# Expert pairs of a two-layer decoder: the four tile sums of the pair before placed behind the up products

## The chip, the cores and the metric

The kernel runs on one core of a Trainium2 chip. The metric is the device time of one execution in microseconds (us), lower is better. Each kernel is timed several times and the median is given; one further execution was recorded by the hardware profiler. The engines are TensorE (PE, with its weight loads shown as PEld), VectorE (DVE), ScalarE (ACT), GpSimd (POOL) and SyncE (SP), which issues the weight transfers.

## What is computed

Two decoder layers over 512 tokens of width 1024. Each layer has a token mixer (a gated linear recurrence in layer 0, sparse attention in layer 1), and then a mixture of 32 experts of which each token uses two. The change touches the experts alone. Cut to what matters:

```python
D_MODEL, SEQ, N_EXPERTS, TOP_K_IN_GROUP, D_EXPERT = 1024, 512, 32, 2, 512

def expert_block(args):
    xb, e = args
    return (jax.nn.silu(xb @ w_gate[e]) * (xb @ w_up[e])) @ w_down[e]

# x = x + sum over the token's two experts of gate * expert(rms_norm(x))
y = grouped_swiglu(xt, eid, w_gate, w_up, w_down).reshape(N, TOP_K_IN_GROUP, D)
out = jnp.sum(y * gate[..., None].astype(y.dtype), axis=1)
```

Every expert's weights are three matrices of 2 MiB in float32 (gate and up 1024x512, down 512x1024), so one layer reads 192 MiB of expert weights.

## The kernel before

**Pairs.** The experts of a layer are worked on in 16 pairs (`NP`), with up to 64 tokens (`CAP`) of each expert. The two experts sit in the two halves of the 128 partitions of PSUM. In each pair TensorE does: the gate product (`both` with `BANK_GATE`, 32 matmul records on L1646), the up product (`both` with `BANK_UP`, L1646), the transposes of the hidden values (`hidden_T`, L1654, 4 records), the transposes of the next pair's tokens (`tokens_T`, L1635, 8 records), and the down product (`down` on L1664, in the first two pairs of a layer `down_half` on L1673). In between it adds the outputs of the pair before to the tokens that they belong to: `combine` (L1682) multiplies a one-hot matrix with the outputs, split into three bf16 parts, for each of the four 128-token tiles: 6 matmuls of 512 columns per tile, 24 in all. `combine_of` does several tiles. They are written to PSUM banks 4 and 5 for tiles 0 and 2, banks 6 and 7 for tiles 1 and 3.

**VectorE.** `add_of` and `add_tile` (L2321) add each tile from PSUM to `x` in SBUF, and count `c_added`. A tile's matmuls wait until the tile two before it, which used the same banks, has been added. `hidden` (L2304) multiplies the up product with the silu of the gate product and counts `h_done`, for which `hidden_T` waits. `tokens_out` (L2298), `one_hot` (L2308) and the splitting of the outputs (L2314, L2317) come behind that.

**ScalarE.** It does the silu (L1188), copies the transposed hidden values to SBUF (L1192), for which the down product waits (`ht_sbuf`), and makes two of the three parts of the output.

**Weights.** SyncE's queue brings the six matrices of a pair (gate, up, down, of two experts each) into ten slots of `arena`, in the order in which they are used. A transfer into a slot is issued when the product that read the slot has finished (`slot_released`: `gate_psum`, `up_psum` or `y_psum`). The gate matrices of a pair go into the slots of the up matrices of two pairs before, the up matrices into those of the down matrices of two pairs before, the down matrices into those of the gate matrices of the pair before. For pairs 1 and 2 (the first twelve transfers beyond the ten slots) and again for the last two pairs of a layer, each matrix comes in two halves: L585 and L589. In the last two pairs the product waits for the second half at its middle (`late`), in the down product after a quarter.

**Ends.** In a layer's last pair there are no tokens to transpose. Its outputs are added behind the pair by the matmuls on L1756 and VectorE's L2365.

The order of every engine is written out by hand; nothing reorders it. The main loop of TensorE is unrolled, VectorE's pairs 2 to 14 run in a loop.

Of the kernel before, what the change touches and what calls it, by code (L numbers as in the profile page):

```python
# [283 lines left out]
def hybrid_trunk(nc, a, out):  # L284
# [8 lines left out]
    with ExitStack() as ctx:  # L293
# [198 lines left out]
        def wait_alone(eng, s, value):  # L492

            eng.wait_ge(s, value)
            eng.nop(nofuse=True)
# [4 lines left out]
        def wait_emptied(eng, name):  # L500
            who, n = jobs.emptied(name)
            eng.wait_ge(emptied[who], n)
# [40 lines left out]
        def landed_at(L, q):  # L543

            per_layer = [[32 if given_back_by_halves(v) else 16 for v in range(u, 6 * NP, NU)] for u in range(NU)]
            return L * sum(per_layer[q % NU]) + sum(per_layer[q % NU][:q // NU + 1])
# [688 lines left out]
        def _(pe):  # L1235
# [42 lines left out]
            for L in range(2):  # L1278
# [339 lines left out]
                def banks_emptied():  # L1618

                    n = jobs.number[f"{L}.first.1"]  # L1620
                    for who in ("act", "dve"):
                        pe.wait_ge(emptied[who], jobs.before[n][who])

                def table():
                    b = open_bank(f"{L}.table")
                    pe.wait_ge(placed, L + 1)
                    for k in range(2):
                        for t in range(NT):
                            ins = pe.matmul(b[:, 0:2 * NE], place_hot[:, k, t].rearrange("p c n -> p (c n)"),
                                            expert_pay[:, k, t].rearrange("p c e -> p (c e)"), start=k + t == 0, stop=k + t == NT)  # L1630
                    ins.then_inc(filled, 1)

                def tokens_T(s_, n=P):
                    for k in range(KD):
                        ins = pe.transpose(ps[:, BANK_XT[k // 4], (k % 4) * P:(k % 4) * P + n], xg[0:n, k::KD][:, 0:P], ident[0:n, 0:n])  # L1635
                    ins.then_inc(s_, 1)

                def both(bank, units, s_, spread=None, half=None, late=None):

                    for k in range(KD):  # L1640
                        if spread and k % 4 == 0:
                            wait_emptied(pe, spread[k // 4])
                        if late and k == KD // 2:
                            pe.wait_ge(late, 32 * (L + 1))
                        for e, u in enumerate(units):
                            ins = pe.matmul(ps[e * CAP:(e + 1) * CAP, bank, :], tokT[:, k, e * CAP:(e + 1) * CAP], rows_in[u][:, k, :],  # L1646
                                            start=k == 0, stop=k == KD - 1)
                        if half and k == KD // 2 - 1:
                            ins.then_inc(half, 1)
                    ins.then_inc(s_, 1)  # L1650

                def hidden_T(s_, n=P):
                    for j in range(KF):
                        ins = pe.transpose(ps[:, BANK_HT, j * P:j * P + n], h_sb[0:n, j::KF][:, 0:P], ident[0:n, 0:n])  # L1654
                    ins.then_inc(s_, 1)
# [22 lines left out]
                def combine(t, s_, part=slice(0, P)):  # L1678

                    for c in range(2):  # L1680
                        for q, y in enumerate(y_parts):
                            ins = pe.matmul(ps[:, 4 + 2 * (t % 2) + c, :], onehot[part, t * P:(t + 1) * P], y[part, c, :],  # L1682
                                            start=q == 0, stop=q == 2)
                    ins.then_inc(s_, 1)

                def combine_of(n, ts, started=True):

                    for t in ts:
                        if t == 0:
                            pe.wait_ge(m["y_mid"], n * 2 + 2)  # L1690
                            pe.wait_ge(m["y_low"], n * 2 + 2)
                            pe.wait_ge(m["g_done"], n + 1)
                        if started or t >= 2:
                            pe.wait_ge(m["c_added"], n * NT + (t - 1))
                        combine(t, m["c_psum"])

                def pair(p):

                    n, first, last = NP * L + p, p == 0, p == NP - 1
                    turned = (NP - 1) * L + p  # L1700
                    units = [(6 * p + j) % NU for j in range(6)]
                    half = half_read if p < 2 else None
                    late = [second_half[3 * (p - NP + 2) + v] if p >= NP - 2 else None for v in range(3)]

                    def weights_of(kind):
                        for j in (2 * kind, 2 * kind + 1):
                            pe.wait_ge(landed[units[j]], landed_at(L, 6 * p + j))

                    weights_of(0)
                    if first:  # L1710
                        for name in (f"{L}.rank.1", f"{L}.fT.{NT - 1}.0"):
                            wait_emptied(pe, name)
                        both(BANK_GATE, units[0:2], m["gate_psum"], [f"{L}.first.{h}" for h in range(2)], half=half)
                        banks_emptied()
                        table()
                    else:
                        pe.wait_ge(m["xt_sbuf"], turned * 2)
                        both(BANK_GATE, units[0:2], m["gate_psum"], half=half, late=late[0])
                        combine_of(n - 1, (0, 1), n > 1)
                    weights_of(1)  # L1720
                    both(BANK_UP, units[2:4], m["up_psum"], half=half, late=late[1])
                    if not first:
                        combine_of(n - 1, (2, 3))
                    wait_alone(pe, m["h_done"], n + 1)
                    hidden_T(m["ht_psum"])
                    if not first:
                        pe.wait_ge(m["c_added"], n * NT - 1)
                        if not last:
                            wait_alone(pe, gathered, (turned + 1) * 16)
                            tokens_T(m["xt_psum"])  # L1730
                    weights_of(2)
                    pe.wait_ge(m["ht_sbuf"], n + 1)
                    if first:
                        wait_emptied(pe, f"{L}.table")
                    if p >= 2:
                        down(units[4:6], m["y_psum"], late[2])
                        return
                    down_half(units[4:6], 0, (None, half))
                    if first:
                        wait_alone(pe, gathered, (turned + 1) * 16)  # L1740
                        tokens_T(m["xt_psum"])
                    down_half(units[4:6], 1, (m["y_psum"], m["y_psum"]))
# [47 lines left out]
        def _(dve):  # L1790
# [40 lines left out]
            for L in range(2):  # L1831
# [475 lines left out]
                def one_hot(c, s_, part=slice(0, P)):  # L2307
                    dve.tensor_scalar(onehot[part, :], iota_tok[part, :], c[part, 0:1], None, ALU.is_equal).then_inc(s_, 1)  # L2308
# [14 lines left out]
                def add_of(n, ts, started=True):  # L2323
                    for t in ts:
                        dve.wait_ge(m["c_psum"], n * NT + (t + 1))
                        if started:
                            dve.wait_ge(m["c_added"], n * NT + (t - 3))
                        add_tile(t, m["c_added"])

                def pair(n, p, first=False, second=False, last=False):  # L2330
                    dve.tensor_copy(cur[:], tabP[:, p, :] if isinstance(p, int) else
                                    tabP[:, bass.ds(p, 1), :].rearrange("p a b -> p (a b)")).then_inc(cur_ready, 1)
                    if not first:
                        add_of(n + (-1), (0, 1), not second)
                    dve.wait_ge(cur_ready, n + 1)
                    dve.wait_ge(m["up_psum"], n + 1)
                    dve.wait_ge(m["silu_done"], n + 1)
                    hidden(cur[:], m["h_done"])
                    if not first:
                        add_of(n + (-1), (2, 3), not second)  # L2340
                    if not last:
                        tokens_out(m["xt_psum"], n + (1 - L), m["xt_sbuf"])
                    one_hot(cur[:], m["g_done"])
                    if last:
                        last_split(n)
                    else:
                        split(m, n)
# [81 lines left out]
```

## Time and profile before

| | us |
|---|---|
| median of 3 runs | 1440.76 |
| lowest and highest | 1437.71, 1442.62 |
| the profiled execution | 1437.13 |
| its span in the trace | 1435.3 |
| TensorE (PE) busy | 1377.1 (96% of the span) |
| VectorE busy | 593.2 (41%) |
| ScalarE busy | 329.5 (23%) |

The span runs from the first to the last recorded instruction; 1.8 us lie around it. The profiled execution is 3.6 us under the median. TensorE worked at its full clock nearly everywhere (mean granted clock 0.997). The expert pairs of layer 0 run from about 253 to 711 us of the span and those of layer 1 from about 972 to the end. The kernel reads 457.41 MB from HBM.

### The profile page before, as it was taken

What the parts mean: (1) busy time and instruction counts of PE and PEld (TensorE: products, weight loads), DVE (VectorE), ACT (ScalarE), POOL (GpSimd) and SP (SyncE); (2) the same over time, 40 slices, a digit from 0 to 9 for tenths busy, and PEclk for the clock granted to TensorE, in tenths of its full rate; (3) what the DMA queues carried; (4) which work ended last, traced back from release to release, by engine and by line L of the source; (5) the groups of instructions that cost most, each with busy time, mean ns of one, the idle gap of its engine ahead of it and who ended that gap; (6) DMA issues with size and microseconds to landing.
All of it is one profiled execution on the core that took longest, in us unless ns stands there. A gap on an engine that the chain in (4) does not pass through costs nothing.

```text
span 1435.3 us, 16528 instructions
## 1 busy us (share of the span) xinstructions
PE 1377.1 (96%) x6368; PEld 619.6 (43%) x6433; DVE 593.2 (41%) x1112; ACT 329.5 (23%) x644; POOL 98.5 (7%) x191
## 2 busy tenths in 40 slices
PE   7999999999999999999899989999999999999997
PEld 3464466433333333333354555564343333333332
DVE  4655104434333333333539864244343333333333
ACT  4455002111111110111326764221111101100111
POOL 1001000200000000000000223003000000000000
PEclk9999999999999999999999999999999999999999
DMA  8207394999999999999930030699999999999995
GB/s 289 109 0 231 114 355 175 365 423 426 426 427 428 426 427 428 427 422 421 352 100 1 1 122 1 231 348 353 421 428 427 426 428 424 429 428 426 423 420 238
DMA packets 73999, 457.26 MB, mean 319 GB/s; under 512 B 15884, under 2 KB 23628, under 8 KB 43848
## 3 DMA queue, kind: packets, MB, share of 16 engines
q1 hardware_dynamic: 68160, 447.97, 76.6%
q0 software_dynamic: 4928, 8.22, 1.5%
q8 instruction: 53, 0.87, 0.2%
q10 hardware_dynamic: 840, 0.06, 0.0%
q14 instruction: 18, 0.15, 0.0%
HBM read 457.41 MB, written 10.53 MB: 326 GB/s over the span
## 4 chain that ended last, share of the span: by engine, by line
PE 70%; DMA 9%; SPq 8%; DVE 7%; ACT 3%; issue 2%; POOL 0%; DVEq 0%; ACTq 0%
PE ps L1646 22%; PE ps L1259 17%; PE ps L1664 11%; PE ps L1682 8%; DMA arena<-in_moe_w_up 5%; SPq L585 5%; DMA arena<-in_moe_w_down 4%; SPq L589 3%; PE ps L1673 2%; PE ps L1635 2%; DVE mix L1984 1%; DVE small L1983 1%; PE ps L1561 1%; PE ps L1520 1%; PE ps L1654 1%
## 5 line engine op out<-in xcount | busy, mean ns | idle before, releaser
L1646 PE MATMUL ps<-arena,xT 128*64 128x512 f32 x2048 | 454.5, 596 | 14.0 <-issue 11.3
L1646 PEld LDWEIGHTS ps<-arena,xT 128*64 128x64 f32 x2048 | 149.5, 137 | 298.5 <-issue 293.5
L2321 DVE TENSOR_TENSOR x<-ps,x 128x1024 f32<-128x1024 f32 x120 | 146.5, 1224 | 204.3 <-PE ps L1682 202.0
L1664 PE MATMUL ps<-arena,xT 128*64 128x512 f32 x896 | 199.1, 596 | 2.2 <-ACT xT L1192 1.6
L1259 PE MATMUL ps<-xT,arena 128*128 128x512 f32 x384 | 169.0, 595 | 1.7 <-DVE xT L1817 1.3
L1682 PE MATMUL ps<-mix,xT 128*128 128x512 bf16 x660 | 157.4, 379 | 6.4 <-issue 4.6
L1682 PEld LDWEIGHTS ps<-mix,xT 128*128 128x128 bf16 x720 | 65.5, 98 | 119.5 <-issue 48.7
L1664 PEld LDWEIGHTS ps<-arena,xT 128*64 128x64 f32 x896 | 61.8, 137 | 118.4 <-issue 112.0
L1259 PEld LDWEIGHTS ps<-xT,arena 128*128 128x128 f32 x384 | 71.9, 190 | 91.2 <-issue 88.5
L1192 ACT ACTIVATE xT<-ps 128x512 f32<-128x512 f32 x32 | 19.1, 597 | 390.6 <-PE ps L1654 390.6
L1259 PE MATMUL ps<-arena,mix 128*128 128x512 f32 (+1 forms) x256 | 105.6, 568 | 0.0
L2314 DVE TENSOR_TENSOR mix<-ps,mix 128x512 f32<-128x512 f32 x60 | 41.5, 691 | 151.9 <-ACT mix L1198 151.9
L2304 DVE SCALAR_TENSOR_TENSOR xT<-ps,cur,xT 128x512 f32<-128x512 f32 x32 | 24.0, 751 | 180.3 <-PE ps L1646 175.6
L1198 ACT ACTIVATE mix<-ps 128x512 bf16<-128x512 f32 x60 | 35.8, 597 | 204.8 <-PE ps L1664 175.3
L1259 PEld LDWEIGHTS ps<-arena,mix 128*128 128x128 f32 x256 | 47.9, 190 | 49.9 <-issue 48.8
L811 POOL CAST whole<-tabP 128x1 int32 (+1 forms) x30 | 5.7, 192 | 865.9 <-PE ps L1635 676.0
L1188 ACT ACTIVATE xT<-ps 128x512 f32<-128x512 f32 x32 | 19.1, 597 | 179.4 <-PE ps L1646 179.4
L804 POOL TENSOR_SCALAR arena<-arena,small 128x256 f32<-128x256 f32 (+3 forms) x80 | 39.4, 512 | 250.5 <-DVE small L1999 181.1
L1826 DVE TENSOR_TENSOR x<-ps,x 128x512 f32<-128x512 f32 x16 | 11.1, 692 | 92.5 <-PE ps L1259 89.4
L2298 DVE TENSOR_TENSOR xT<-ps,gains 128x512 f32<-128x512 f32 x60 | 38.6, 686 | 17.0 <-PE ps L1635 13.1
L2317 DVE TENSOR_TENSOR mix<-mix 128x512 bf16<-128x512 f32 x60 | 41.2, 687 | 2.9
L1201 ACT ACTIVATE mix<-mix 128x512 bf16<-128x512 f32 x60 | 37.5, 626 | 7.2 <-DVE mix L2314 7.2
(281 smaller groups left out, 1181.8 us busy)
## 6 DMA issues: line engine op xcount, KB each, us to landing
arena<-in_moe_w_gate SPq DMA_DIRECT2D x48, 2048.0 KB, 27.4
arena<-in_moe_w_up SPq DMA_DIRECT2D x48, 2048.0 KB, 26.2
arena<-in_moe_w_down SPq DMA_DIRECT2D x48, 2048.0 KB, 30.0
arena<-in_moe_w_down SPq DMA_DIRECT2D x32, 1024.0 KB, 20.6
arena<-in_moe_w_gate SPq DMA_DIRECT2D x32, 1024.0 KB, 21.4
arena<-in_moe_w_up SPq DMA_DIRECT2D x32, 1024.0 KB, 21.4
arena<-in_w_out SPq DMA_DIRECT2D x4, 2048.0 KB, 11.2
arena<-in_dsa_w_in SPq DMA_DIRECT2D x1, 5120.0 KB, 17.6
```

Of the source, the lines that this page charges most:

```text
L585: sp.dma_start(rows_in[u][:, ks, :], src[:, ks, :]).then_inc(done, 16)
L589: sp.dma_start(rows_down[u][:, js, :], src[:, js, :]).then_inc(done, 16)
L804: ins = pool.tensor_scalar(buf[:, h, 0:width], buf[:, h, 0:width], inv[:, h:h + 1], 1.0, ALU.mult, ALU.mult)
L1201: act.activation(y_mi[part, c, :], y_rest[part, c, :], ACT.Copy).then_inc(q["y_mid"], 1)
L1259: ins = pe.matmul(b[part, cols], l, r, start=i == 0, stop=i == len(pairs) - 1)
L1646: ins = pe.matmul(ps[e * CAP:(e + 1) * CAP, bank, :], tokT[:, k, e * CAP:(e + 1) * CAP], rows_in[u][:, k, :], start=k == 0, stop=k == KD - 1)
L1664: ins = pe.matmul(ps[e * CAP:(e + 1) * CAP, BANK_Y + c, :], hT[:, j, e * CAP:(e + 1) * CAP], rows_down[u][:, j, c * 512:(c + 1) * 512], st ...
L1682: ins = pe.matmul(ps[:, 4 + 2 * (t % 2) + c, :], onehot[part, t * P:(t + 1) * P], y[part, c, :], start=q == 0, stop=q == 2)
L2298: dve.tensor_tensor(tokT[:, 4 * q:4 * q + 4, :], ps[:, BANK_XT[q], :].rearrange("p (k n) -> p k n", k=4), gains[:, 3 * L + 2, 4 * q:4 * q ...
L2314: dve.tensor_tensor(y_rest[part, c, :], ps[part, BANK_Y + c, :], y_hi[part, c, :], ALU.subtract).then_inc(q["y_rest"], 1)
L2317: dve.tensor_tensor(y_lo[part, c, :], y_rest[part, c, :], y_mi[part, c, :], ALU.subtract).then_inc(q["y_low"], 1)
L2321: dve.tensor_tensor(x[:, t, :], ps[:, b:b + 2, :].rearrange("p a n -> p (a n)"), x[:, t, :], ALU.add).then_inc(s_, 1)
```

## The change

On TensorE the tiles 0 and 1 of the pair before move from between the gate and the up product to behind the up product, ahead of tiles 2 and 3. On VectorE the additions of tiles 0 and 1 move behind `hidden`. Nothing is added or removed.

```diff
--- before.py
+++ after.py
@@ -1716,10 +1716,10 @@
                     else:
                         pe.wait_ge(m["xt_sbuf"], turned * 2)
                         both(BANK_GATE, units[0:2], m["gate_psum"], half=half, late=late[0])
-                        combine_of(n - 1, (0, 1), n > 1)
                     weights_of(1)
                     both(BANK_UP, units[2:4], m["up_psum"], half=half, late=late[1])
                     if not first:
+                        combine_of(n - 1, (0, 1), n > 1)
                         combine_of(n - 1, (2, 3))
                     wait_alone(pe, m["h_done"], n + 1)
                     hidden_T(m["ht_psum"])
@@ -2330,13 +2330,12 @@
                 def pair(n, p, first=False, second=False, last=False):
                     dve.tensor_copy(cur[:], tabP[:, p, :] if isinstance(p, int) else
                                     tabP[:, bass.ds(p, 1), :].rearrange("p a b -> p (a b)")).then_inc(cur_ready, 1)
-                    if not first:
-                        add_of(n + (-1), (0, 1), not second)
                     dve.wait_ge(cur_ready, n + 1)
                     dve.wait_ge(m["up_psum"], n + 1)
                     dve.wait_ge(m["silu_done"], n + 1)
                     hidden(cur[:], m["h_done"])
                     if not first:
+                        add_of(n + (-1), (0, 1), not second)
                         add_of(n + (-1), (2, 3), not second)
                     if not last:
                         tokens_out(m["xt_psum"], n + (1 - L), m["xt_sbuf"])
```

TensorE's order in the last pair of layer 0, from the gate product's second half to the transposes of the hidden values, before (the names in brackets are the semaphores waited for; `second_half4` is the landing of the up matrices' second half):

```order
L1646 MATMUL ps<-arena,xT 64x512 x7
L1682 MATMUL ps<-mix,xT 128x512 [waits g_done,c_added,y_low,y_mid]
L1682 MATMUL ps<-mix,xT 128x512 x5
L1682 MATMUL ps<-mix,xT 128x512 [waits c_added]
L1682 MATMUL ps<-mix,xT 128x512 x5
L1646 MATMUL ps<-arena,xT 64x512 [waits landed3,landed2]
L1646 MATMUL ps<-arena,xT 64x512 x7
L1646 MATMUL ps<-arena,xT 64x512 [waits second_half4]
L1646 MATMUL ps<-arena,xT 64x512 x7
L1682 MATMUL ps<-mix,xT 128x512 [waits c_added]
L1682 MATMUL ps<-mix,xT 128x512 x5
```

The same place in the changed kernel:

```order
L1646 MATMUL ps<-arena,xT 64x512 x7
L1646 MATMUL ps<-arena,xT 64x512 [waits landed3,landed2]
L1646 MATMUL ps<-arena,xT 64x512 x7
L1646 MATMUL ps<-arena,xT 64x512 [waits second_half4]
L1646 MATMUL ps<-arena,xT 64x512 x7
L1682 MATMUL ps<-mix,xT 128x512 [waits g_done,c_added,y_low,y_mid]
L1682 MATMUL ps<-mix,xT 128x512 x5
L1682 MATMUL ps<-mix,xT 128x512 [waits c_added]
L1682 MATMUL ps<-mix,xT 128x512 x5
L1682 MATMUL ps<-mix,xT 128x512 [waits c_added]
L1682 MATMUL ps<-mix,xT 128x512 x5
```

The block of tiles 0 and 1 has gone from ahead of the up product to behind it, and tile 2, which waits for the addition of tile 0, now follows it at once.

VectorE's order in the last pair of layer 0, as a difference between the two kernels (in the rest of the loop it is the same move):

```order
 L2331 COPY cur<-tabP 128x2
-L2321 TENSOR_TENSOR x<-ps,x 128x1024 [waits c_added,c_psum] x2
 L2304 SCALAR_TENSOR_TENSOR xT<-ps,cur,xT 128x512 [waits silu_done,up_psum,cur_ready]
-L2321 TENSOR_TENSOR x<-ps,x 128x1024 [waits c_added,c_psum] x2
+L2321 TENSOR_TENSOR x<-ps,x 128x1024 [waits c_added,c_psum] x4
 L2308 TENSOR_SCALAR xT<-iota_tok,cur 128x512
```

All four additions now stand behind the hidden product of L2304.

## Rows read from the trace of the kernel before

**Rows 1.** The page's slices: DMA busy tenths and GB/s, 40 slices of 35.9 us

```profile
DMA  8207394999999999999930030699999999999995
GB/s 289 109 0 231 114 355 175 365 423 426 426 427 428 426 427 428 427 422 421 352 100 1 1 122 1 231 348 353 421 428 427 426 428 424 429 428 426 423 420 238
```

**Rows 2.** Windows: busy us of PE, PEld, DVE, ACT, POOL, PEclk, DMA share, GB/s

```profile
240.00:260.00 20.00, 19.70 (x133) 13.70 (x131) 12.14 (x47) 4.91 (x8) 0.00 (x0) 1.00 0.65 240
300.00:320.00 20.00, 19.84 (x96) 7.19 (x97) 7.51 (x11) 3.41 (x6) 1.20 (x2) 1.00 1.01 419
```

**Rows 3.** The page's DMA issues: count, KB of one, median us to landing

```profile
arena<-in_moe_w_down SPq DMA_DIRECT2D x48, 2048.0 KB, 30.0
```

**Rows 4.** Timeline of PE, pair 5 of layer 0: start us, us, what, idle before

```profile
390.56 7.04 PE L1646 MATMUL ps<-arena,xT 128*64 128x512 f32 x32
397.76 2.54 PE L1682 MATMUL ps<-mix,xT 128*128 128x512 bf16 x11 [0.16 <-issue]
400.22 7.09 PE L1646 MATMUL ps<-arena,xT 128*64 128x512 f32 x32
407.24 2.76 PE L1682 MATMUL ps<-mix,xT 128*128 128x512 bf16 x11
409.84 0.63 PE L1654 MATMUL ps<-ident,xT 128*128 128x128 f32 x4
...
411.30 7.09 PE L1664 MATMUL ps<-arena,xT 128*64 128x512 f32 x32
418.22 2.31 PE L1646 MATMUL ps<-arena,xT 128*64 128x512 f32 x10
```

**Rows 5.** Timeline of DVE in the same pair

```profile
399.12 2.52 DVE L2321 TENSOR_TENSOR x<-ps,x 128x1024 f32<-128x1024 f32 x2 [5.56 <-PE ps L1682]
407.42 0.75 DVE L2304 SCALAR_TENSOR_TENSOR xT<-ps,cur,xT 128x512 f32<-128x512 f32 x1 [5.77 <-PE ps L1646]
408.84 2.43 DVE L2321 TENSOR_TENSOR x<-ps,x 128x1024 f32<-128x1024 f32 x2 [0.67 <-PE ps L1682]
```

**Rows 6.** Timeline of pair 0, where TensorE waits for VectorE

```profile
269.26 0.75 DVE L2304 SCALAR_TENSOR_TENSOR xT<-ps,cur,xT 128x512 f32<-128x512 f32 x1 [2.29 <-issue]
...
270.16 0.72 PE L1654 MATMUL ps<-ident,xT 128*128 128x128 f32 x4 [1.01 <-DVE xT L2304]
```

**Rows 7.** Timeline of PE, layer 0: gate product of pair 12, gate and up of 13

```profile
588.22 7.09 PE L1646 MATMUL ps<-arena,xT 128*64 128x512 f32 x32 [2.19 <-issue]
...
618.72 7.09 PE L1646 MATMUL ps<-arena,xT 128*64 128x512 f32 x32 [2.03 <-issue]
...
629.16 7.09 PE L1646 MATMUL ps<-arena,xT 128*64 128x512 f32 x32 [0.67 <-DMA arena<-in_moe_w_up]
```

**Rows 8.** Timeline of PE and PEld, last pair of layer 0

```profile
686.16 7.33 PE L1646 MATMUL ps<-arena,xT 128*64 128x512 f32 x32
...
689.83 0.20 PEld L1646 LDWEIGHTS ps<-arena,xT 128*64 128x64 f32 x4 [0.90 <-DMA arena<-in_moe_w_up]
...
693.42 2.76 PE L1682 MATMUL ps<-mix,xT 128*128 128x512 bf16 x11
...
696.02 0.63 PE L1654 MATMUL ps<-ident,xT 128*128 128x128 f32 x4
```

**Rows 9.** The same timeline, down product of that pair and what follows

```profile
697.43 1.94 PE L1664 MATMUL ps<-arena,xT 128*64 128x512 f32 x8 [0.78 <-ACT xT L1192]
699.68 5.37 PE L1664 MATMUL ps<-arena,xT 128*64 128x512 f32 x24 [0.31 <-DMA arena<-in_moe_w_down]
704.98 2.76 PE L1756 MATMUL ps<-mix,xT 128*128 128x512 bf16 x11
```

**Rows 10.** Timeline of PE, last pair of layer 1

```profile
1411.44 2.76 PE L1682 MATMUL ps<-mix,xT 128*128 128x512 bf16 x11
...
1415.45 1.94 PE L1664 MATMUL ps<-arena,xT 128*64 128x512 f32 x8 [0.78 <-ACT xT L1192]
1417.66 5.37 PE L1664 MATMUL ps<-arena,xT 128*64 128x512 f32 x24 [0.27 <-DMA arena<-in_moe_w_down]
```

## The prediction, made before the changed kernel ran

> **What bounds the kernel now.** I read the page's slices first. TensorE looks full (96%), but so does the DMA: in both stretches of expert pairs nearly every slice has 9 tenths and about 427 GB/s [rows 1]. The windows of 20 us say when it starts: share 0.65 from 240 to 260 us, and 1.01 with 419 GB/s from 300 to 320 [rows 2]. So from pair 0 on the transfers run without a pause, and the time of their last landing is set by bytes over rate, not by TensorE.
>
> The timeline of a pair shows how close TensorE is to that. In pair 5 it never waits: from gate product to gate product 418.22 - 390.56 = 27.66 us [rows 4]. The stream needs more for a pair. In pair 13 the gate product waits 2.03 us and the up product 0.67 us [rows 7]. Gate products 12 and 13, which both wait, start 618.72 - 588.22 = 30.5 us apart [rows 7]. So TensorE starts a layer with ten loaded slots, works faster than they are refilled, and meets the stream at pair 11: by its own pace that gate product would come at 418.22 + 5 x 27.66 = 556.5 us, by the stream's at 588.22 - 30.5 = 557.7. From there each product starts when its weights land.
>
> The last pair is therefore the place that counts. The second half of the up matrices lands at 689.83 us, TensorE goes on at once, and tiles 2 and 3 start 3.59 us later, at 693.42 us [rows 8]. Behind them stand the transposes (696.02 us), ScalarE's copy, and the down product at 697.43 us. That reaches its first wait after a quarter and goes on at 699.68 us, when the last weights of the layer have landed [rows 8, 9]. A product takes 704.98 - 699.68 = 5.30 us for three quarters, so a quarter is 1.77 us. TensorE was ready for the last landing at 697.43 + 1.77 = 699.20 us and had **0.48 us to spare**. In layer 1 it is 1417.66 - 1415.45 - 1.77 = 0.44 us [rows 10]. Whatever is put between the last up product and the last down product beyond this half microsecond is paid in full.
>
> **The change, part by part.**
>
> Pairs 1 to 14, TensorE. Two tiles leave the place between gate and up and come back behind up: 400.22 - 397.76 = 2.46 us gone, 2.60 us (407.24 to 409.84) added, and the gap of 0.16 us before the first tile goes along with it [rows 4]. What is new is that tile 2 follows tile 1 at once and needs the banks of tile 0. VectorE starts adding tile 0 1.36 us after the first tile's matmuls start (397.76 to 399.12) and takes 1.26 us (2.52 for two) [rows 4, 5]. TensorE sees the end of a VectorE operation about 0.15 us later (269.26 + 0.75 to 270.16) [rows 6]. So tile 2 can start 1.36 + 1.26 + 0.15 = 2.77 us after tile 0 did, and the two tiles fill 2.54 us: a wait of 0.23 us. Tile 3 needs tile 1's addition, which ends 1.26 us after tile 0's, while tile 2's matmuls take 1.27 us: no second wait. I take 0.23 us; the bounds are 0 and 1.26, a whole addition laid open.
>
> Trainium skill, Perfetto Trace Analysis, section Optimizing Tensor Performance: independent matmul groups should rotate through different banks so that the evacuation of one overlaps the matmuls of the next. By that rule alone two pairs of banks would hide each addition and the wait would be zero, which takes 0.5 us off the sum below; the rows above leave 0.23 us per pair.
>
> VectorE's product for the hidden values comes 0.18 us after the up product and takes 0.75 us [rows 5], so it is done before the first tile is complete; putting it ahead of the additions delays nobody. The transposes, which wait for it, now have four tiles ahead of them instead of two.
>
> A pair thus takes 27.66 + 0.23, about 27.9 us, still under the stream's 30.5. Over ten pairs TensorE comes some 2 us later to the stream and gains 2.6 us in each pair behind it. Cost: nothing, as long as the stream never runs dry. The slots of the up matrices come free 2.5 us earlier, those of the down matrices up to 2 or 3 us later. A transfer of two matrices lasts about 9.8 us (689.83 to 699.67, [rows 8, 9]) and the median from issue to landing of a down matrix is 30.0 us [rows 3]: some 20 us of work stand ahead of it in the queue, more than the lateness. In the first pairs the queue is shorter, but so is the lateness (0.23 us for each pair).
>
> Last pair, TensorE. Does the up product still end when it did? The up product of pair 13 starts with its weights at 629.16 us [rows 7]; two pairs of 27.9 us later is 684.96, its half is done at 688.5, 1.3 us before the second half lands at 689.83. So its end stays at 693.42 us, tied to the landing. Behind it now stand 0.16 + 2 x 2.60 + 0.23 = 5.59 us instead of 2.60: **2.99 us more**. The 0.48 us to spare is used up, so the down product starts 2.99 us later, finds all its weights, and ends 2.99 - 0.48 = 2.51 us later. What it would do without the slack is 2.99, with no wait for an addition 2.28.
>
> In layer 1 the down matrices' second half lands at 1417.66 us; 9.84 us before that, 1407.82, plus 3.59 is 1411.41, against 1411.44 in the row [rows 10]. So here too the up product cannot end earlier, and the sum is 2.99 - 0.44 = 2.55, less the 0.03: 2.52 us.
>
> What follows the pairs (L1756, the last additions, in layer 0 the whole of layer 1) hangs on the end of the down product, and moves with it. Nothing on POOL's or SP's queue is moved; the next tokens are fetched once per pair as before.
>
> Sum: 2.51 + 2.52 = **5.0 us more**. Against the profiled execution's own 1437.13 us that is 1442.1. The runs' median is 3.6 us above it and I lay the sum on that: 1440.76 + 5.0 = **1445.8 us**, 0.35% slower. With no wait and with 0.5 us more wait for each of the two blocks the sum is 4.6 and 6.0.
>
> **Rivals.**
>
> *Hidden after all (not slower).* In the last pair there are 0.48 us to spare because the last two transfers land 9.84 us apart. If in the executions that make up the median the last down matrices came 3 us later after the up matrices than in the profiled one, the four tiles would vanish behind them. For it: the median run is 3.6 us longer, somewhere. Against: both layers show the same slack, 0.48 and 0.44 us, and a stream that is slow everywhere stretches 9.84 us by hundredths. It decides at 3.0 us; the time would be 1440.8 to 1443.
>
> *The additions hold TensorE up in every pair (much slower).* If tiles 2 and 3 each wait longer, say 1 us per pair in all, ten pairs make 10 us, TensorE reaches pair 11 some 9 us behind the stream (it came there 1.2 us ahead), and regains only 30.5 - 28.7 = 1.8 us per pair, 7 in four. Then it is late at the last up product too. It decides at about 0.8 us per pair; at 1 us each layer loses 3.0 + 0.8 - 0.5 + 2, some 5.5 us, so about 1452. Against it: VectorE's additions are as quick as the tiles (1.26 against 1.27 us).
>
> *A faster stream (faster).* The gate matrices are asked for 2.5 us earlier. The most that could give is the lack of rate in the first windows, 427 - 419 GB/s over some 40 us, 0.7 us in each layer [rows 2]. With the above it leaves +3.6 us, 1444.4. Only if the tail's cost is wrong as well would the kernel get faster.
>
> **How the numbers follow.** The forecast has 0.72, hidden 0.12, much slower 0.10, faster stream 0.06. A measurement of this kernel can tell about 0.3%, 4.3 us, from no change. The forecast's 4.6 to 6.0 lies just above that, and medians of a few runs with a spread of 5 us move by 1 to 2: two in three that it shows as slower, one in three as same. So slower is 0.48 + 0.10, and a little of the last, 0.59; same is 0.24 + 0.11 + 0.02, 0.37; faster 0.04. The range takes the forecast with its bounds and scatter and part of each neighbour: 1441 to 1449.5.
>
> **What would show it right or wrong.** In the changed kernel's timeline: gate to gate 27.9 us in pairs 2 to 10; a wait of some 0.2 us inside the 24 matmuls of L1682; the wait before the up product in pairs 11 to 13 grown to about 2 us and that before the gate product shrunk; DMA share still 1.0 with the last landing at the same place; the last down product with no wait for its weights, starting 7.0 us behind the end of the up product instead of 4.0, with L1756 2.5 us later in layer 0 and 5 us later in layer 1. It is wrong if the last down product still waits for its weights, if the DMA pauses in pairs 1 to 4, or if the additions cost TensorE over 0.8 us per pair.

## The result, and the profile after

| | us |
|---|---|
| changed kernel, median of 9 runs | 1445.72 (1442.90 to 1448.43) |
| kernel before, median of 9 runs | 1440.82 (1437.58 to 1443.23) |
| ratio of the two | 1.0035, 95% interval 1.0025 to 1.0045 |
| profiled execution of the changed kernel | 1442.90, span 1441.1 |

The change costs 5.0 us (3.6 to 6.5 by the interval). The predicted time was 1445.8 us. Here and below the ratio is an estimate from all runs of both kernels and not the quotient of the two medians, so the two can differ by 0.1%; a cost in us is worked out from the ratio.

The page's slices show the same picture as [rows 1]: the DMA is as full, and moves as much.

```profile
DMA  8207294999999999999830030698999999999995
GB/s 285 111 0 228 105 363 173 359 422 427 426 426 428 424 428 427 427 422 421 341 98 1 1 122 1 222 351 357 422 427 426 427 428 426 426 427 427 424 420 216
```

The window from 300 to 320 us, to set beside [rows 2] (busy us of PE, PEld, DVE, ACT and POOL, granted clock, DMA share, GB/s):

```profile
300.00:320.00 20.00, 20.00 (x101) 7.78 (x101) 6.67 (x10) 3.54 (x6) 1.21 (x2) 1.00 1.01 420
```

So the transfers run from pair 0 to the last weights with no slice in which they pause, before and after.

TensorE's timeline in pair 9 of layer 0, a pair without a wait for weights, answers to [rows 4]:

```profile
503.08 13.90 PE L1646 MATMUL ps<-arena,xT 128*64 128x512 f32 x64
516.92 5.64 PE L1682 MATMUL ps<-mix,xT 128*128 128x512 bf16 x24
522.39 0.63 PE L1654 MATMUL ps<-ident,xT 128*128 128x128 f32 x4
...
523.85 7.09 PE L1664 MATMUL ps<-arena,xT 128*64 128x512 f32 x32
530.77 7.04 PE L1646 MATMUL ps<-arena,xT 128*64 128x512 f32 x32
```

Gate and up product are now one run of 64 records, the four tiles one run of 24. From gate to gate it is 530.77 - 503.08 = 27.69 us, where before had 27.66: only 0.03 us more. The 0.03 is a difference of two terms. The four tiles take 522.39 - 516.92 = 5.47 us, which is 0.25 more than the 2.62 and 2.60 us of the two blocks before (from the end of the gate product at 397.60 to 400.22, and 407.24 to 409.84 [rows 4]). Gate and up product take 13.84 us in one run, where before they took 7.04 + 7.02 = 14.06 in two.

VectorE's timeline in pair 5, to set beside [rows 5]. The hidden product comes 0.17 us after the first tile starts behind the up product (406.16), then two additions, a pause, and two more:

```profile
406.33 0.75 DVE L2304 SCALAR_TENSOR_TENSOR xT<-ps,cur,xT 128x512 f32<-128x512 f32 x1 [11.00 <-PE ps L1646]
407.76 2.52 DVE L2321 TENSOR_TENSOR x<-ps,x 128x1024 f32<-128x1024 f32 x2 [0.67 <-PE ps L1682]
410.63 2.43 DVE L2321 TENSOR_TENSOR x<-ps,x 128x1024 f32<-128x1024 f32 x2 [0.36 <-PE ps L1682]
```

In the pairs that wait for weights the wait has moved from ahead of the gate product [rows 7] to ahead of the up product, here in pair 12 of layer 0; before it, gate follows down at once:

```profile
590.98 7.04 PE L1646 MATMUL ps<-arena,xT 128*64 128x512 f32 x32
600.75 7.09 PE L1646 MATMUL ps<-arena,xT 128*64 128x512 f32 x32 [2.73 <-DMA arena<-in_moe_w_up]
```

The last pair of layer 0, PE, PEld and one row of VectorE, answers to [rows 8, 9]:

```profile
692.05 3.65 PE L1646 MATMUL ps<-arena,xT 128*64 128x512 f32 x16 [1.23 <-DMA arena<-in_moe_w_up]
695.63 5.55 PE L1682 MATMUL ps<-mix,xT 128*128 128x512 bf16 x24
...
697.14 2.52 DVE L2321 TENSOR_TENSOR x<-ps,x 128x1024 f32<-128x1024 f32 x2 [0.58 <-PE ps L1682]
698.42 0.98 PEld L1682 LDWEIGHTS ps<-mix,xT 128*128 128x128 bf16 x6 [0.52 <-DVE x L2321]
...
699.71 0.98 PEld L1682 LDWEIGHTS ps<-mix,xT 128*128 128x128 bf16 x6 [0.32 <-DVE x L2321]
...
701.02 0.63 PE L1654 MATMUL ps<-ident,xT 128*128 128x128 f32 x4
...
702.43 7.09 PE L1664 MATMUL ps<-arena,xT 128*64 128x512 f32 x32 [0.78 <-ACT xT L1192]
...
709.45 2.76 PE L1756 MATMUL ps<-mix,xT 128*128 128x512 bf16 x12
```

The reader is to see three things. The up product still waits for its second half (1.23 us), so it ends where the landing lets it. The four tiles take 701.02 - 695.63 = 5.39 us. And the down product is one run of 32 records: it no longer waits for the last weights.

The last pair of layer 1 is the same, beside [rows 10]:

```profile
1411.34 3.65 PE L1646 MATMUL ps<-arena,xT 128*64 128x512 f32 x16 [1.10 <-DMA arena<-in_moe_w_up]
1414.93 5.55 PE L1682 MATMUL ps<-mix,xT 128*128 128x512 bf16 x24
...
1421.73 7.09 PE L1664 MATMUL ps<-arena,xT 128*64 128x512 f32 x32 [0.78 <-ACT xT L1192]
1428.75 2.76 PE L1756 MATMUL ps<-mix,xT 128*128 128x512 bf16 x12
```

**The tail** is the stretch from the landing of the last up weights to the first matmul of L1756. It was 704.98 - 689.83 = 15.15 us in layer 0; it is 709.45 - 692.05 = 17.40 and 1428.75 - 1411.34 = 17.41 us. In layer 1 of the kernel before no wait marks the landing, but the trace has the landing events themselves, 0.04 us ahead of the first matmul that uses the weights. From them the tail is 15.19 and 15.23 us before and 17.45 in both layers after: 2.26 and 2.22 us more, 4.5 in all.

The difference of the two spans, 5.8 us, splits like this. Pair 0 of layer 0 starts 1.73 us later (254.84 against 253.11), in front of anything that was changed. Nearly all of that is one product, here before and after, which took 8.69 instead of 7.10 us behind the same wait, at a granted clock of 0.66 in the window from 14 to 18 us against 1.00 before:

```profile
15.35 7.10 PE L1259 MATMUL ps<-xT,arena 128*128 128x512 f32 x16 [1.34 <-DVE xT L1817]
...
15.49 8.69 PE L1259 MATMUL ps<-xT,arena 128*128 128x512 f32 x16 [1.34 <-DVE xT L1817]
```

From pair 0 to L1756 it is 454.61 us against 451.87, 2.74 more; the stretch from there to pair 0 of layer 1 is the same to 0.01 us; the pairs of layer 1 take 452.14 against 450.83, 1.31 more. The tails have 2.26 each of these; the rest, +0.5 and -0.9, is when the last up weights land: 0.48 us later and 0.91 us earlier, counted from pair 0. Shifts of this size come without any change of order: the four traces in which all pairs but the last have the order of before have the last weights of layer 0 land between 446.45 and 447.45 us after the start of pair 0, and those of layer 1 between 444.81 and 445.65.

### The profile page after: what moved, and what is told of

The parts are those of the page before. It is cut to its first block, busy times and chain, and to the rows that moved or that the text cites. A ratio compares the mean times of both kernels' runs of the same rounds, so it can differ in the third digit from the quotient of the medians.

```text
span 1441.1 us, 16593 instructions
## 1 busy us (share of the span) xinstructions
PE 1384.6 (96%) x6433; PEld 621.0 (43%) x6433; DVE 593.3 (41%) x1112; ACT 329.5 (23%) x644; POOL 98.8 (7%) x191
## 3 DMA queue, kind: packets, MB, share of 16 engines
q1 hardware_dynamic: 68160, 447.97, 76.3%
## 4 chain that ended last, share of the span: by engine, by line
PE 66%; DMA 14%; DVE 9%; SPq 6%; ACT 3%; issue 1%; POOL 0%; DVEq 0%; ACTq 0%
PE ps L1646 19%; PE ps L1259 17%; DMA arena<-in_moe_w_up 14%; PE ps L1664 10%; PE ps L1682 7%; SPq L585 4%; PE ps L1673 2%; DVE x L2321 2%; DVE mix L1984 1%; SPq L589 1%; PE ps L1635 1%; DVE small L1983 1%; PE ps L1561 1%; PE ps L1520 1%; PE ps L1654 1%
## 5 line engine op out<-in xcount | busy, mean ns | idle before, releaser
L2304 DVE SCALAR_TENSOR_TENSOR xT<-ps,cur,xT 128x512 f32<-128x512 f32 x32 | 24.0, 751 | 357.3 <-PE ps L1646 352.7
L1682 PE MATMUL ps<-mix,xT 128*128 128x512 bf16 x720 | 165.8, 380 | 3.0
```

## Experiments

The first theory: the cost sits in the last pair of each layer alone, in the tail. The rival: the other pairs pay, by additions that hold TensorE up or slots that come free later. Times are medians; the ratio is against runs of the kernel before on the same chip, made next to them.

### The last pair alone

```diff
-                        combine_of(n - 1, (0, 1), n > 1)
+                        combine_of(n - 1, () if last else (0, 1), n > 1)
...
-                        combine_of(n - 1, (2, 3))
+                        combine_of(n - 1, (0, 1, 2, 3) if last else (2, 3), n > 1)
```

and the same two conditions in VectorE's `add_of`.

> The change in the last pair of each layer alone, on both engines; all other pairs as in the kernel before. Tail theory (the whole cost is the longer block between the last up and the last down product): L1756 starts 17.4 us after the last up weights land, as in the changed kernel (before: 15.15), and the time rises by all of the change's cost, 4.5 to 5.0 us. Rival (the cost comes from the 14 other pairs, by additions that hold TensorE up or by slots that come free later and slow the stream): within 1 us of before.

Measured: 1443.52 against 1440.14 us, ratio 1.0028 (1.0017 to 1.0039), which is 4.0 us (2.4 to 5.6). The timeline of PE, last pair of layer 0:

```profile
689.77 3.65 PE L1646 MATMUL ps<-arena,xT 128*64 128x512 f32 x16 [1.23 <-DMA arena<-in_moe_w_up]
693.36 5.55 PE L1682 MATMUL ps<-mix,xT 128*128 128x512 bf16 x24
...
700.16 7.09 PE L1664 MATMUL ps<-arena,xT 128*64 128x512 f32 x32 [0.78 <-ACT xT L1192]
707.18 2.76 PE L1756 MATMUL ps<-mix,xT 128*128 128x512 bf16 x12
```

The tail is 707.18 - 689.77 = 17.41 us, and 17.41 in layer 1. The time moved by most of the whole change. The tail theory holds for this pair.

### All pairs but the last

The same lines with the condition turned round: all four tiles behind in pairs 1 to 14, the last pair as before.

> The change in all pairs but the last of each layer. Tail theory: no difference, within 1 us of before, although each of these pairs takes 0.1 to 0.2 us longer on TensorE; the last down product still waits for its weights. Rival (the other pairs or the stream pay): 4.5 to 5 us more, or whatever part of it the first experiment lacks. A faster stream through the up slots that come free earlier would show as up to 2 us less than before.

Measured: 1443.38 against 1440.14 us, ratio 1.0020 (1.0011 to 1.0029): 2.9 us more. The tail theory said that nothing would change, so it **fell** as the whole story. The last pair of layer 1 shows that TensorE comes late there, since its down product runs through without a wait for weights, which [rows 10] had:

```profile
1349.82 8.78 PE L1646 MATMUL ps<-arena,xT 128*64 128x512 f32 x32 [2.12 <-DMA arena<-in_moe_w_up]
...
1420.78 7.09 PE L1664 MATMUL ps<-arena,xT 128*64 128x512 f32 x32 [0.78 <-ACT xT L1192]
1427.80 2.55 PE L1756 MATMUL ps<-mix,xT 128*128 128x512 bf16 x11
```

The first row is the up product of pair 13. From its start to L1756 there is not one wait for weights left: 77.98 us of TensorE work, of which the slow product (8.78 instead of 7.09 us, see below) has 1.7. Without it that is 76.3; in layer 0, where the up product of pair 13 ran at the full clock, it is 76.28 (631.27 to 707.55 us), again with no wait in it. In the kernel before, the up product of pair 13 in layer 0 started at 629.16 us [rows 7], and L1756 75.82 us later, with waits in between. So with the four tiles behind the up product the same landing is followed by more work than the stream leaves time for.

That gave a second theory, **phase**: in the pairs that wait for weights, the two tiles between gate and up filled time in which the weights of the up product had not yet landed. Moved behind the up product, they are done after the wait instead of in it, and by the theory TensorE reaches the last pair up to 2.6 us later.

### One tile

```diff
-                        combine_of(n - 1, (0, 1), n > 1)
+                        combine_of(n - 1, (0,) if last else (0, 1), n > 1)
...
-                        combine_of(n - 1, (2, 3))
+                        combine_of(n - 1, (1, 2, 3) if last else (2, 3), n > 1)
```

> In the last pair of each layer tile 0 stays ahead of the up product and tile 1 alone moves behind it; all else as before. Tail theory: the block behind the up product is 3 tiles and a wait of 0.2 us, some 4.0 us instead of 2.6, the half microsecond to spare is used up first, so 0.9 to 1.0 us for each layer, 1.8 to 2.0 in all: well under half of the whole change's cost. Rival (each moved tile costs the same, with no slack): 2.5 us, half of it. Rival (a threshold that only the second moved tile passes): 0.

Measured: 1442.51 against 1440.14 us, ratio 1.0014 (1.0003 to 1.0025): 2.0 us. The tail is 453.75 - 437.64 = 16.11 us in layer 0 and 450.94 - 434.83 = 16.11 in layer 1 (times from the start of pair 0), 0.96 more than before's 15.15. One tile costs 0.96 us in a layer, two cost 2.26. The second costs its whole 1.30 us; the first is cheaper, since the half microsecond to spare is taken off it and only the wait for an addition (0.2 us) put on. In time the interval (0.4 to 3.6 us) is too wide to part 1.9 from 2.5; the traces do.

### TensorE's order alone

Both blocks moved on TensorE, the additions of tiles 0 and 1 left ahead of the hidden product on VectorE.

> TensorE's order as in the changed kernel, VectorE's as in the kernel before: the additions of tiles 0 and 1 ahead of the hidden product. The hidden values are then ready 1.6 + 2.5 + 0.75 = 4.85 us after the up product, and the four tiles take 5.4 to 5.5, so the transposes don't wait. Theory: the same time as the changed kernel, 4.5 to 5 us over before. Rival (VectorE's order carries part of the cost or saves some): over 1 us away from that.

Measured: 1445.78 against 1440.14 us, ratio 1.0031 (1.0020 to 1.0043): 4.5 us, with a tail of 454.71 - 437.31 = 17.40 us in layer 0. In layer 1 the up product of pair 13 ran at the lower clock (8.78 us), TensorE came to the last pair late, and its up product ran through without a wait; by the landing event the tail there is 18.01 us, 0.56 more. VectorE's order carries nothing that can be seen in the time. The trace shows a little: in pair 9 the stretch from the tiles to the down product takes 523.79 - 516.67 = 7.12 us, against 523.85 - 516.92 = 6.93 in the changed kernel, since the hidden product now stands between the additions of tiles 1 and 2, and the transposes of the tokens (L1635) wait for that of tile 2. So the two experiments that follow, made on TensorE alone, carry some 0.2 us for each pair that the whole change does not have.

```profile
516.67 5.64 PE L1682 MATMUL ps<-mix,xT 128*128 128x512 bf16 x24
...
522.72 1.14 PE L1635 MATMUL ps<-ident,mix 128*128 128x128 f32 x8
523.79 7.09 PE L1664 MATMUL ps<-arena,xT 128*64 128x512 f32 x32
```

### Where among the other pairs

The four tiles behind the up product in pairs 1 to 10 alone, and in pairs 11 to 14 alone:

```diff
-                        combine_of(n - 1, (0, 1), n > 1)
+                        combine_of(n - 1, () if 1 <= p <= 10 else (0, 1), n > 1)
...
-                        combine_of(n - 1, (2, 3))
+                        combine_of(n - 1, (0, 1, 2, 3) if 1 <= p <= 10 else (2, 3), n > 1)
```

> TensorE's order changed in pairs 1 to 10 of each layer, in which TensorE works from loaded slots; pairs 11 to 15 and VectorE as in the kernel before. Theory A (phase): the four-tile block costs only where the stream sets the pace, because there the two tiles no longer fill the wait ahead of the up product; here nothing, within 1 us of before. Theory B (each pair pays a little, or slots that come free later or earlier disturb the stream): the 2.9 us of the second experiment or most of it.

> TensorE's order changed in pairs 11 to 14 alone, where TensorE waits for weights. Theory A (phase): TensorE reaches the last pair 2 to 3 us later than before and uses up what it had to spare there; worked out from the landings of the trace before, 0.4 to 0.9 us for each layer, and 2 for a layer in which a product of pair 12 or 13 runs at the lower clock (8.78 instead of 7.09 us): 1.3 to 3 us in all, the same as the second experiment's 2.9. The last down product waits for its weights little or not at all. Theory B (early pairs pay): within 1 us of before.

Measured: pairs 1 to 10 give 1440.09 against 1441.42 us, ratio 0.9995 (0.9985 to 1.0006), nothing. Pairs 11 to 14 give 1445.08, ratio 1.0021 (1.0008 to 1.0034): 3.0 us (1.2 to 4.9), the same as pairs 1 to 14 together. So the ten early pairs are free and the four that wait for weights carry what there is, and not a little from each pair. The trace of the second, layer 1, from the up product of pair 13:

```profile
1352.46 7.09 PE L1646 MATMUL ps<-arena,xT 128*64 128x512 f32 x32 [1.93 <-DMA arena<-in_moe_w_up]
...
1422.07 7.09 PE L1664 MATMUL ps<-arena,xT 128*64 128x512 f32 x32 [0.78 <-ACT xT L1192]
1429.09 1.25 PE L1756 MATMUL ps<-mix,xT 128*128 128x512 bf16 x5
```

76.63 us without a wait, here at the full clock all through. The 0.35 us over the 76.28 of the experiment with both engines is the 0.2 us that VectorE's order costs in each of two pairs. How much of the 3.0 us is the order itself is read from how late L1756 starts behind the last landing, in the table at the end of this section: 0.82 and 0.74 us more than before, 1.6 us in all. The last weights landed 0.68 and 0.48 us later than before, within what landings scatter; whether the order has a part in that, one trace can't tell. So the rest of the 3.0 stays open. The runs' granted clock points at one part of it: the five of the twelve runs with a mean granted clock of 0.991 to 0.993 took 1445.4 to 1446.5 us, the seven with 0.994 or 0.995 took 1440.7 to 1445.2, and the kernel before was at 0.993 to 0.997.

### How much TensorE work the stream hides

```diff
-                    for c in range(2):
+                    for c in [0, 1] * times:
...
+                        combine(t, m["c_psum"], times=2 if twice and t == 3 else 1)
...
+                        combine_of(n - 1, (2, 3), twice=2 <= p <= 13)
```

> The order of before, with the six matmuls of tile 3 done twice in pairs 2 to 13 (the same values again): 1.27 us more of TensorE work in each of 12 pairs, 15.2 us for each layer. Theory (the stream sets the end, and TensorE has waits of some 8 us in a layer to give): 5 us for each layer and 1.7 more where a product runs at the lower clock, 10 to 13 us in all, so a third of the 30.5 us of added work. Rival (TensorE's work sets the end): 30 us. Rival (the stream hides it all): 0.

Measured: 1452.19 against 1441.42 us, ratio 1.0073 (1.0054 to 1.0092): 10.5 us for 30.5 us of added work. In both layers no product from pair 1 on waits for weights. Two thirds of the work vanished in waits, the rest is in the time. This also puts a number to the second rival of the prediction: of work spread over pairs 2 to 13 behind the up product, some 10 us per layer are free.

### A tile in ScalarE's gap

```diff
-                        combine_of(n - 1, (2, 3))
+                        combine_of(n - 1, (2,) if last else (2, 3))
                     wait_alone(pe, m["h_done"], n + 1)
                     hidden_T(m["ht_psum"])
+                    if last:
+                        combine_of(n - 1, (3,))
```

> The order of before, but in the last pair of each layer tile 3 is done behind the transposes of the hidden values, where TensorE otherwise waits 0.78 us for ScalarE's copy. The last down product can then start 0.8 to 0.9 us earlier. Theory: its wait for the last weights grows from 0.3 to 1.1 us and the end stays where it is, as long as TensorE isn't late; where a product in pairs 12 to 15 ran at the lower clock TensorE is late and gains up to 0.8 us. So 0 to 1 us less than before. Rival (TensorE's chain sets the end in both layers): 1.6 us less.

Measured: 1441.99 against 1441.42 us, ratio 1.0001 (0.9990 to 1.0013), no difference. The down product of the last pair of layer 1 (L1758 is the line that is L1756 in the other kernels):

```profile
1417.69 1.94 PE L1664 MATMUL ps<-arena,xT 128*64 128x512 f32 x8
1420.75 5.37 PE L1664 MATMUL ps<-arena,xT 128*64 128x512 f32 x24 [1.12 <-DMA arena<-in_moe_w_down]
1426.06 2.76 PE L1758 MATMUL ps<-mix,xT 128*128 128x512 bf16 x12
```

The wait grew from 0.27 us [rows 10] to 1.12, by just what was saved. In the order of before it is the landing that ends the layer, and time given to TensorE there is worth nothing.

### One tile ahead in the waiting pairs

In pairs 11 to 14 tile 0 ahead of the up product and three behind it.

> TensorE's order: in pairs 11 to 14 of each layer tile 0 ahead of the up product and tiles 1 to 3 behind it; all other pairs, the last too, and VectorE as before. The waits for weights in these pairs should then split into some 1.9 us ahead of the up product and 0.8 us ahead of the gate product, instead of 0.5 and 2.0 (before) or 2.7 and 0 (all four behind). Phase theory: TensorE reaches the last pair 1.3 us later than before and 1.3 us earlier than with all four behind, so the last down product starts without a wait, or nearly so, and the cost is 0 to 0.5 us for each layer, under 1 us in all, as long as no product runs at the lower clock. If the low clock after waits of 2 us and more is what cost the sixth experiment half of its 3 us, then no product of 8.6 to 8.8 us should be seen here, and the time be within 0.5 us of before or up to 1 us under it. Rival (the cost rises evenly with each tile moved in these pairs): 1.5 us more.

Measured: 1442.19 against 1440.39 us, ratio 1.0003 (0.9992 to 1.0014), no difference that can be told. The wait before the gate product was there in pair 11 alone; in pairs 12 and 13 of layer 0 all of it, 2.3 us, stood ahead of the up product, against what was expected. None of the pairs' products ran slow. The run can't tell whether fewer slow products help, since its interval is wider than that.

The pairs take 452.31 and 451.23 us from pair 0 to L1756, 0.44 and 0.40 more than before. That is not TensorE coming late, for the last weights landed 0.44 and 0.35 us later too, and landings scatter by more than that where the order is the same. The table takes the landing out. Its first numbers are the landing of a layer's last weights, counted from the start of pair 0, and the second ones how long after it the first matmul of L1756 starts, each for layers 0 and 1, in us:

| kernel | last landing | L1756 behind it |
|---|---|---|
| before | 446.52, 445.48 | 5.35, 5.35 |
| changed kernel | 447.02, 444.74 | 7.59, 7.40 |
| last pair alone | 446.45, 445.57 | 7.61, 7.36 |
| pairs 1 to 14 | 446.81, 446.08 | 5.88, 7.33 |
| one tile, last pair | 447.45, 444.81 | 6.30, 6.14 |
| TensorE's order alone | 447.08, 445.78 | 7.63, 7.98 |
| pairs 1 to 10 | 447.91, 446.12 | 5.35, 5.35 |
| pairs 11 to 14 | 447.20, 445.96 | 6.17, 6.09 |
| a tile in the gap | 446.59, 445.65 | 5.35, 5.35 |
| one tile ahead | 446.96, 445.83 | 5.35, 5.40 |

5.35 us is the shortest there is: the three quarters of the down product that need the last weights, and the 0.04 us from the landing to a matmul. So one of the two tiles moved in pairs 11 to 14 costs nothing to 0.05 us in a layer and both cost 0.7 to 0.8: a part that is free and then the full price, as in the last pair. The 7.33 of pairs 1 to 14 and the 7.98 of TensorE's order alone are the layers in which the up product of pair 13 ran at the lower clock. And the changed kernel's numbers are those of the last pair alone: with the last pair changed, the other pairs add nothing.

None of the versions beats the kernel before, and the traces say why: its two tiles behind the last up product leave TensorE 0.5 us early for the last landing, so neither fewer tiles there (the gap experiment) nor more pays.

## Why the prediction was right, step by step

**The stream sets the end of each layer.** Right: slices and window after are those of before, the early pairs are free, and 30.5 us of extra work cost 10.5.

**The up product of the last pair ends with its landing, and what comes behind is a chain on TensorE.** Right: 1.23 and 1.10 us of wait for its second half after, and a tail of the same length in both layers and in the experiment on the last pair alone.

**Size of the tail.** 2.51 us predicted, 2.26 measured. The block of four tiles takes 5.39 us, not 5.59; another 0.05 us comes from the down product, 7.02 us in one run against the 1.77 + 5.30 of the sum. The term that was mis-sized is the "gap of 0.16 us before the first tile" that I had go along: those rows have 11 records of 12 matmuls, and the one that is missing from the trace is the first. It was no wait. In the changed kernel's trace all 24 are there and there is no gap. The wait for the additions was put at 0.23 us; by the block, 5.39 - 2 x 2.60, it is 0.19. All of it stands ahead of tile 2: that starts 698.42 - 695.63 = 2.79 us after tile 0, and two tiles fill 2.60. The weight loads of tile 3 wait for VectorE too (0.32 us of PEld's row), but they start 699.71 - 698.42 = 1.29 us after those of tile 2, a tile's own length, so this wait holds no matmul up, as predicted. That 0.23 came so near is in part luck, since its terms were off both ways: the first addition starts 697.14 - 695.63 = 1.51 us after the tile and not 1.36, it takes 1.22 and not 1.26, TensorE goes on 0.06 us after it and not 0.15, and two tiles fill 2.60 us, not the 2.54 of a row with a record missing.

The rule of the Trainium skill (Perfetto Trace Analysis, Optimizing Tensor Performance) on rotating through banks, by which no wait would be left, was nearly met: two pairs of banks for additions of 1.22 us and tiles of 1.30 us leave 0.2 us in 5.4.

**The other pairs.** "Cost: nothing, as long as the stream never runs dry" held for the change as a whole, and the working behind it was right: the prediction followed TensorE through these pairs and found it at the middle of the last up product 1.3 us ahead of the landing, and 1.23 was measured. The 27.9 us for a pair were 27.69; that the 24 matmuls take longer was foreseen, that gate and up in one run are 0.22 us shorter was not. But the sentence is too wide as it stands: it gives the stream as the only condition, and there is a second one, that the last pair changes too. In pairs 11 to 14 the same change alone costs 3.0 us (1.2 to 4.9), of which the table shows 1.6, though the stream didn't run dry, because two tiles left ahead of the last up product are then in the way of a TensorE that comes late. That also says why the two halves of the change, 4.0 and 2.9 us, make 5.0 together and not 6.9: in the whole change all four tiles are behind the last up product, so it is on time for its landing again, and the lateness of the other pairs costs nothing more than the tail does. The table bears this out, with 7.59 and 7.40 us for the whole change and 7.61 and 7.36 for the last pair alone.

**The sum.** 5.0 us predicted and 5.0 measured is in part luck: the tails are 4.5, and the interval of the measurement goes from 3.6 to 6.5. What the other 0.5 us is, if it isn't the scatter, the runs don't settle. A likely cause, which is not shown, is more products at the lower clock: the mean granted clock of the nine runs is 0.9936, that of the kernel before in 27 runs made later, on another occasion, 0.9951.

**The rivals.** *Hidden after all*: no, TensorE is late for the last landing in both layers. *Additions hold TensorE up*: 0.27 us per pair (5.47 - 2 x 2.60), far from 0.8, and the net lengthening is 0.03. Its own sum was off a little, 3.0 + 0.8 - 0.5 + 2 being 5.3 and not 5.5. *Faster stream*: the last up weights land 0.5 us later and 0.9 us earlier than before, so nothing of one sign.

## What to carry to other kernels

When a stream of transfers sets the pace, work on the fast engine is free as long as it stands ahead of a wait, and paid in full behind the last one: ask of each moved block which wait it filled, not how long it is. Follow the engine through the last few stages with the landings held fixed, since two moves that each cost a few us alone can share the same slack. When traces are compared, take the landing out first: the last landing of layer 0 was 1.4 us later in the trace of pairs 1 to 10, whose runs show no cost, so only what comes behind the landing tells of the order. And before a small idle time in a trace is put into a sum, count the records: eleven rows of twelve mean that the gap may be the missing one.

## What the hardware showed that was not expected

TensorE's clock falls after waits of about 2 us, in some cases and not in others. The up product of pair 11 in layer 1 of the changed kernel is one; the last three columns of the windows are the granted clock, the DMA share and GB/s:

```profile
1291.00:1293.00 2.00, 1.86 (x6) 0.70 (x8) 0.00 (x0) 0.00 (x0) 0.00 (x0) 0.71 1.04 442
1293.00:1295.00 2.00, 2.00 (x8) 0.88 (x6) 0.00 (x0) 0.00 (x0) 0.00 (x0) 0.50 0.94 401
```

TensorE is idle for 2.13 us, starts, and is granted 0.50, the lower of its two levels (1.2 instead of 2.4 GHz), in the second window. The product takes 8.78 us where the others take 7.09, 1.7 more:

```profile
1291.14 8.78 PE L1646 MATMUL ps<-arena,xT 128*64 128x512 f32 x32 [2.13 <-DMA arena<-in_moe_w_up]
```

The trace of before has one such product among the pairs (behind 2.00 us idle), the changed kernel two, that of pairs 1 to 14 three, that of pairs 11 to 14 two, those with the last pair alone, one tile and TensorE's order alone one each, and those with pairs 1 to 10, with one tile ahead, with the extra work and with the tile in the gap none. The Trainium skill (TensorE: Matmul & The Clock Gate, HAM oscillation) tells of the same: a wait for data between two runs of matmuls lets the clock fall and the next run starts at the lower level. The traces agree in kind, with 1.7 us per case; that waits of 2.3 and 2.7 us also passed without it, and that the product at 15.4 us ran slow in some traces and not in others behind the same 1.34 us of idle time, shows that length alone doesn't decide.

What such a product costs depends on where it stands. The one in pair 13 of the kernel before cost nothing: the last down product still waited for its weights. In TensorE's order alone one in pair 13 made the tail 0.56 us longer, and in pairs 1 to 14 it is the difference between 5.88 us in layer 0 and 7.33 in layer 1. Ahead of the pairs it is paid in full: pair 0 starts at 253.1 to 253.2 us in the five traces that have none at the lower clock up to there, and at 254.6 to 255.0 in the six that have one. So part of the scatter of the runs, some 5 us for each kernel, comes in steps of some 1.7 us from parts that no experiment touched. That a product at the lower clock is the whole of each step was seen in the one above (8.69 against 7.10 us) and is assumed for the rest. Whether the changed order makes the clock fall more often, and moves the median by it, was not isolated.
